# Eight 128-wide projection tiles of a two-layer hybrid block, each pair by seven block products in place of eight

## The reference

```
hn = rms_norm_2(x, norm_mix)
proj = einsum('bsd,dc->bsc', hn, w_in)
qa, ka, va, cq, ckv, kr, hc, bc, cc = split(proj)   # 384 384 384 256 128 32 256 256 256
out_a = neighbourhood_attention(norm(qa), norm(ka), va, rpb)
out_b = mla_attention(...)                # from cq, ckv, kr
out_c = bc * conv3(cc * hc)               # 3-tap convolution over the tokens
x = x + concat(out_a, out_b, out_c) normed @ w_out
x = x + expert_choice_moe(norm(x))        # 16 experts, 64 tokens each, 1024 x 1024 gate, up, down
```

## Time and profile before

| | us |
|---|---|
| median of 3 runs | 2571.51 |
| lowest and highest of them | 2571.41, 2572.59 |
| the profiled execution, its own time | 2575.35 |
| its span in the profile | 2573.5 |
| PE busy in the span | 2480.6 (96%) |
| DVE busy | 1155.5 (45%) |
| ACT busy | 477.0 (19%) |
| mean granted TensorE clock | 0.989 |

### The profile page before, as it was taken

One profiled execution on the slowest core, in us unless ns is written; L12 is line 12 of the kernel. 1 busy time (PEld: TensorE's weight loads), 2 busy tenths in 40 slices (PEclk: granted clock), 3 DMA queues, 4 the chain that ended last, 5 costly groups with the idle time before them and its releaser, 6 DMA issues.

```text
span 2573.5 us, 26561 instructions
## 1 busy us (share of the span) xinstructions
PE 2480.6 (96%) x10783; PEld 1499.0 (58%) x10783; DVE 1155.5 (45%) x2015; ACT 477.0 (19%) x1009; POOL 141.6 (6%) x237
## 2 busy tenths in 40 slices
PE   7999999999999999999999999889999999999899
PEld 3458888888888888555653333333456653333333
DVE  4667888755766643334741222111334641222112
ACT  2332121002222001233710000000224610000000
POOL 1321110000000000001100000000001000000000
PEclk9999999999999999999999999999999999999999
DMA  8535774551434225211159999999420259999998
GB/s 302 206 116 178 266 245 148 155 147 43 133 120 131 66 66 176 87 54 77 59 206 366 427 428 427 427 428 417 151 98 33 73 197 409 428 427 427 427 429 353
DMA packets 187097, 601.77 MB, mean 234 GB/s; under 512 B 8960, under 2 KB 123328, under 8 KB 161632
## 3 DMA queue, kind: packets, MB, share of 16 engines
q1 hardware_dynamic: 169072, 544.59, 54.8%
q0 software_dynamic: 16608, 51.22, 5.8%
q10 hardware_dynamic: 1296, 4.25, 0.4%
HBM read 593.74 MB, written 6.29 MB: 233 GB/s over the span
## 4 chain that ended last, share of the span: by engine, by line
PE 76%; DMA 16%; DVE 6%; issue 1%; SPq 1%; ACT 1%; DVEq 0%; ACTq 0%
DMA arena<-in_w_down 14%; PE ps L2713 9%; PE ps L2144 9%; PE ps L2269 7%; PE ps L2747 7%; PE ps L2381 5%; PE ps L2155 4%; PE ps L2617 4%; PE ps L2113 3%; PE ps L2375 3%; PE ps L2180 2%; PE ps L2038 2%; PE ps L2395 2%; PE ps L2758 2%; PE ps L2060 1%; PE ps L2552 1%
## 5 line engine op out<-in xcount | busy, mean ns | idle before, releaser
L2144 PE MATMUL ps<-arena 128*128 128x256 f32 x1280 | 278.3, 380 | 0.6 <-DVE arena L1300 0.6
L2144 PEld LDWEIGHTS ps<-arena 128*128 128x128 f32 x1280 | 242.5, 190 | 34.6 <-issue 2.0
L2713 PE MATMUL ps<-arena,first 128*64 128x512 f32 x1024 | 231.4, 593 | 12.9 <-DMA arena<-in_w_up 12.9
L2713 PE MATMUL ps<-arena 128*64 128x512 f32 x1024 | 232.4, 595 | 1.3 <-DMA arena<-in_w_up 1.3
L2747 PE MATMUL ps<-arena 128*64 128x512 f32 x896 | 210.5, 628 | 22.6 <-DMA arena<-in_w_down 21.3
L2269 PE MATMUL ps<-arena 128*128 128x256 f32 x896 | 193.8, 379 | 0.1
L2269 PEld LDWEIGHTS ps<-arena 128*128 128x128 f32 x896 | 170.1, 190 | 23.6 <-issue 0.5
L2713 PEld LDWEIGHTS ps<-arena,first 128*64 128x64 f32 x1024 | 73.3, 137 | 162.2 <-issue 136.4
L2747 PEld LDWEIGHTS ps<-arena 128*64 128x64 f32 x896 | 68.1, 144 | 162.2 <-issue 160.4
L2713 PEld LDWEIGHTS ps<-arena 128*64 128x64 f32 x1024 | 73.4, 137 | 139.8 <-issue 131.4
L2155 PE MATMUL ps<-arena 128*128 128x256 f32 x672 | 146.2, 379 | 3.0 <-DVE arena L1358 3.0
(11 more groups left out here) (465 smaller groups left out, 3179.7 us busy)
## 6 DMA issues: line engine op xcount, KB each, us to landing
arena<-in_w_gate SPq DMA_DIRECT2D x64, 2048.0 KB, 37.3
arena<-in_w_up SPq DMA_DIRECT2D x64, 2048.0 KB, 36.0
arena<-in_w_down SPq DMA_DIRECT2D x54, 2048.0 KB, 35.2
arena<-in_ffn_w SPq DMA_DIRECT2D x24, 2048.0 KB, 9.6
arena<-in_w_mod POOLq DMA_DIRECT2D x80, 512.0 KB, 5.3
arena<-in_ffn_w SPq DMA_DIRECT2D x32, 1024.0 KB, 7.9
arena<-in_w_down SPq DMA_DIRECT2D x16, 1024.0 KB, 37.9
arena<-in_w_in SPq DMA_DIRECT2D x10, 1536.0 KB, 11.6
```

The lines of the kernel that those rows point to most:

```text
L2144: ins = mm(ps[:, i % 6, 0:256], src[:, k, P * j:P * j + P], x[:, k, :], start=(k == 0), stop=(k == 3))
L2713: ins = mm(ps[CAP * half:CAP * half + CAP, bank, :], xsT[q][:, k, CAP * (e % 2):CAP * (e % 2) + CAP], wv[:, k, 512 * half:512 * half + 512 ...
```

## The change

Two tiles A and B over eight blocks of 128 input features are one 2 by 2 block product: weights a11 and a12 (the first and last four blocks of A), a21 and a22 (of B), tokens b11, b12, b21, b22 (first and last four blocks of `hnT`, first and last 256 tokens). Before, the pair takes 16 matmuls of 512 columns. After, it takes seven products of four 128x256 matmuls each, 28 in all, and sums formed by DVE. Four pairs in each layer are done so: three of convolution tiles and one of two qa tiles. The third qa tile stays as it was.

- DVE forms four token sums once per layer (`token_sums`, 1024 elements per partition each), and four weight sums per pair (`pair_sums`, 512 elements each).
- ACT copies the first two products of a pair to SBUF (256 wide). DVE combines the seven into the four quarters of the two tiles by seven adds (`pair_out`, 256 wide).
- ACT's 512-wide evictions of the eight tiles go. The squares of the two qa tiles are taken from SBUF.
- The two qa tiles are computed before ka, not after the tables.
- The token sums lie in slot 5 of the ring. So the first load of the output weights into slot 5 waits for the last product of the layer.

```diff
-        CONV_I = (0, 4, 2, 1, 5, 3)
+        PAIRS = ((4, 0, 10, 1), (4, 1, 10, 2), (4, 2, 10, 0), (1, 0, 1, 1))
+        PAIR_BANK = (4, 5, 6, 7, 0, 1, 2, 3, 4, 5, 6, 7, 3, 4, 5, 6, 7, 3, 4, 5, 6, 7, 3, 4, 0, 1, 2, 7)
...
-                if l:
-                    sp.wait_ge(r2_used[5], loads_before(5, LOADS))
-                else:
-                    sp.wait_ge(sm["f2_ps"], F2_BASE[1] + 28)
+                sp.wait_ge(sm["conv_ps"], 28 * l + 28)
                 for i, k in enumerate((6, 0)):
...
+                def pair_parts(p):
+                    if p >= 2:
+                        act.wait_ge(sm["conv_copied"], 16 * l + 4 * (p - 2) + 2)
+                    for i in range(2):
+                        act.wait_ge(sm["conv_ps"], 28 * l + 7 * p + i + 1)
+                        A(pair_q[p % 2][i], ps[:, PAIR_BANK[7 * p + i], 0:256], ACT.Copy).then_inc(sm["q_sb"], 1)
...
+                def token_sums():
+                    dve.wait_ge(sm["fin_done"], 8 * l + 8)
+                    if l:
+                        dve.wait_ge(sm["hn_ready"], 14 * l)
+                    b11, b12, b21, b22 = (hnT[:, k:k + 4, lo:lo + 256] for k in (0, 4) for lo in (0, 256))
...
+                    V.tensor_tensor(t1, b12, b11, sub).then_inc(sm["t_ready"], 1)
+                    dve.wait_ge(sm["t_ready"], done + 1)
+                    V.tensor_tensor(t2, b22, t1, sub).then_inc(sm["t_ready"], 1)
+                    V.tensor_tensor(t3, b22, b12, sub).then_inc(sm["t_ready"], 1)
+                    dve.wait_ge(sm["t_ready"], done + 2)
+                    V.tensor_tensor(t4, t2, b21, sub).then_inc(sm["t_ready"], 1)
...
+                def pair_sums(p):
+                    sa, ja, sb_, jb = PAIRS[p]
+                    for s in (sa, sb_):
+                        dve.wait_ge(r2_in[s], 16 * (l * (R2_LANDS[s] + slot_total(s)) + IN_LANDS[s]))
...
+                    if p < 2:
+                        dve.wait_ge(sm["proj_ps"], 12 * l + 2)
+                    else:
+                        dve.wait_ge(sm["conv_ps"], 28 * l + 7 * (p - 1))
+                    V.tensor_tensor(s1, a21, a22, add).then_inc(sm["ws_ready"], 1)
...
+                def pair_out(p):
...
+                    chain(V.tensor_tensor(u2_, q, product(2), add))
+                    V.tensor_tensor(u3, u2_, product(3), add)
+                    dve.wait_ge(sm["q_sb"], QSB_BASE + 8 * l + 2 * p + 2)
+                    chain(V.tensor_tensor(u4, u2_, p5, add))
+                    V.tensor_tensor(part(1, 1), shaped(u3), shaped(p5), add).then_inc(sm["conv_copied"], 1)
+                    V.tensor_tensor(part(0, 0), shaped(q), shaped(product(4)), add).then_inc(sm["conv_copied"], 1)
+                    V.tensor_tensor(part(1, 0), shaped(u3), shaped(product(5)), sub).then_inc(sm["conv_copied"], 1)
+                    V.tensor_tensor(part(0, 1), shaped(u4), shaped(product(6)), add).then_inc(sm["conv_copied"], 1)
+
+                token_sums()
+                pair_sums(0)
+                pair_sums(1)
                 dve.wait_ge(sm["proj_copied"], 12 * l + 4)
...
                 for j in range(2):
-                    dve.wait_ge(sm["conv_copied"], 6 * l + 3 * j + 3)
+                    pair_out(j)
+                    pair_sums(2 + j)
+                    dve.wait_ge(sm["conv_copied"], 16 * l + 4 * j + 4)
...
-                    V.tensor_tensor(cv[:, 2 + j, :], o, cv[:, 2 + j, :], mul).then_inc(sm["conv_sq"], 1)
+                pair_out(2)
+                dve.wait_ge(sm["conv_copied"], 16 * l + 12)
+                for j in range(2):
+                    V.tensor_tensor(cv[:, 2 + j, :], cv[:, 4 + j, :], cv[:, 2 + j, :], mul).then_inc(sm["conv_sq"], 1)
+                pair_out(3)
...
+                def product_read(n):
+                    p, i = divmod(n, 7)
+                    if i < 2:
+                        pe.wait_ge(sm["q_sb"], QSB_BASE + 8 * l + 2 * p + i + 1)
+                    else:
+                        pe.wait_ge(sm["conv_copied"], 16 * l + 4 * p + max(i - 2, 1))
...
+                def pair(p):
...
+                    for i, (w, x, s_n, t_n) in enumerate(((wa[:, 0:4], lo[:, 0:4], 0, 0), (s1, t1, 1, 1), (s2, t2, 2, 2), (s3, t3, 3, 3),
+                                                          (wa[:, 4:8], lo[:, 4:8], 0, 0), (wb[:, 4:8], t4, 0, 4), (s4, hi[:, 4:8], 4, 0))):
...
+                        for k in range(4):
+                            ins = mm(ps[:, bank, 0:256], w[:, k, :], x[:, k, :], start=(k == 0), stop=(k == 3))
+                        ins.then_inc(sm["conv_ps"], 1)
+
+                for p in range(2):
+                    pair(p)
                 pe.wait_ge(sm["c_normed"], 4 * l + 4)
+                product_read(6)
...
-                for c in range(4, 6):
-                    conv_in(c)
+                for p in range(2, 4):
+                    pair(p)
...
                 w = weights(1, 384)
-                for p in range(3):
...
+                pe.wait_ge(sm["bias_copied"], 6 * l + 2)
+                features(Q_BANK, w, 2 * P).then_inc(sm["q_ps"], 1)
```

More of the change, by code:

```diff
@@ L325, in program @@
         XT_BANK = (0, 4, 1, 6, 2, 3, 5, 7)
-        CONV_I = (0, 4, 2, 1, 5, 3)
+        PAIRS = ((4, 0, 10, 1), (4, 1, 10, 2), (4, 2, 10, 0), (1, 0, 1, 1))
+        PAIR_BANK = (4, 5, 6, 7, 0, 1, 2, 3, 4, 5, 6, 7, 3, 4, 5, 6, 7, 3, 4, 5, 6, 7, 3, 4, 0, 1, 2, 7)
+        QSB_BASE, TC_BASE, WSC_BASE = 14, 25, 92
+        pair_t = [at(20480 + 1024 * i, 1024, "p (k n) -> p k n", k=4) for i in range(4)]
+        pair_s = [[at(lo + 512 * i, 512, "p (k n) -> p k n", k=4) for i in range(4)] for lo in (34464, 42912)]
+        pair_q = [[at(15360 + 512 * j + 256 * i, 256) for i in range(2)] for j in range(2)]
+        pair_u = [at(44960 + 256 * i, 256) for i in range(3)]
         K_BANK, UP_BANK, BIAS_BANK = (3, 0, 1, 2), (4, 5, 6, 0, 1, 2, 3), (6, 0, 1, 2, 3, 4)
-        Q_BANK, V_BANK = (5, 6, 0), (1, 2, 3, 4)
+        Q_BANK, V_BANK = 0, (1, 2, 3, 4)
         T_BANK = (5, 6, 0, 1, 2, 3, 4, 5, 6, 0, 1, 2, 3, 4, 5)
@@ L813, in _ @@
                 root(0, st[:, 24:32], st[:, 16:24])
-                for c in range(4):
-                    conv_in(c)
+                for p in range(2):
+                    pair_parts(p)
                 for i in range(3):
@@ L850, in _ @@
                     ins.then_inc(sm["bias_copied"], 1)
-                for p in range(3):
-                    act.wait_ge(sm["q_ps"], 3 * l + p + 1)
-                    A(qT[:, p, :], ps[:, Q_BANK[p], :], ACT.Copy)
-                    A(sqq[:, p, :], ps[:, Q_BANK[p], :], ACT.Square).then_inc(sm["q_copied"], 1)
+                act.wait_ge(sm["conv_copied"], 16 * l + 16)
+                for p in range(2):
+                    A(sqq[:, p, :], qT[:, p, :], ACT.Square).then_inc(sm["q_copied"], 1)
+                act.wait_ge(sm["q_ps"], l + 1)
+                A(qT[:, 2, :], ps[:, Q_BANK, :], ACT.Copy)
+                A(sqq[:, 2, :], ps[:, Q_BANK, :], ACT.Square).then_inc(sm["q_copied"], 1)
                 root(2, br_, binv)
@@ L1611, in _ @@
                 chain(ins)
+                def token_sums():
[3 more added lines that the diff above has]
+                    b11, b12, b21, b22 = (hnT[:, k:k + 4, lo:lo + 256] for k in (0, 4) for lo in (0, 256))
+                    t1, t2, t3, t4 = pair_t
+                    done = TC_BASE + 4 * l
+                    V.tensor_tensor(t1, b12, b11, sub).then_inc(sm["t_ready"], 1)
[4 more added lines that the diff above has]
+                    V.tensor_tensor(t4, t2, b21, sub).then_inc(sm["t_ready"], 1)
@@ new lines, in pair_sums @@
+                def pair_sums(p):
+                    sa, ja, sb_, jb = PAIRS[p]
+                    for s in (sa, sb_):
+                        dve.wait_ge(r2_in[s], 16 * (l * (R2_LANDS[s] + slot_total(s)) + IN_LANDS[s]))
+                    wa, wb = (ring2[s][:, 0:KC * 384].rearrange("p (k n) -> p k n", k=KC)[:, :, P * j:P * j + P] for s, j in ((sa, ja), (sb_, jb)))
+                    a11, a12, a21, a22 = wa[:, 0:4], wa[:, 4:8], wb[:, 0:4], wb[:, 4:8]
+                    s1, s2, s3, s4 = pair_s[p % 2]
+                    done = WSC_BASE + 16 * l + 4 * p
+                    if p < 2:
[3 more added lines that the diff above has]
+                    V.tensor_tensor(s1, a21, a22, add).then_inc(sm["ws_ready"], 1)
+                    dve.wait_ge(sm["ws_ready"], done + 1)
+                    V.tensor_tensor(s2, s1, a11, sub).then_inc(sm["ws_ready"], 1)
+                    V.tensor_tensor(s3, a11, a21, sub).then_inc(sm["ws_ready"], 1)
+                    dve.wait_ge(sm["ws_ready"], done + 2)
+                    V.tensor_tensor(s4, a12, s2, sub).then_inc(sm["ws_ready"], 1)
@@ new lines, in pair_out, with product, part, shaped @@
+                def pair_out(p):
+                    def product(n):
+                        dve.wait_ge(sm["conv_ps"], 28 * l + 7 * p + n + 1)
+                        return ps[:, PAIR_BANK[7 * p + n], 0:256]
+                    def part(tile, half):
```

(45 more changed lines are left out.)

16 lines of the change are left out of this document (3 added, 13 removed).

## The result

The changed kernel takes 2557.07 us, median of 4 runs (2554.82 to 2559.69), where the kernel before takes 2571.95 (4 runs, 2571.41 to 2572.59). The ratio is 0.9942 by the medians; that of the runs themselves is 0.9937, 95% interval 0.9926 to 0.9949. The gain is 14.9 us; the forecast was 13.0, at 2558.5, with 2554.5 to 2563.5 as its range.

What follows compares the result with a forecast made beforehand. PE time was taken to bound the changed stretch, with DVE, ACT and DMA costs covered. Eight pairs at 1.62 us saved give 13.0 us, from 2571.51 to 2558.5 us on the median; range 2554.5 to 2563.5.

Steps and rivals of the forecast that it cites:

- Products: Convolution and qa pairs: 56 x 216.3 = 12.11 us a pair, 1.62 saved; four pairs in two layers, 13.0 us.
- Restart at each product: Rival, chance 0.04: seams between the 56 products make PE wait, at 0.58 us each 32.5 us, giving 2591.
- DVE cover: Some 29 us of sums per layer on DVE cost nothing; tightest slack 3.6 us, before the qa pair's first product.
- The rival's price: DVE late by more than its slack in pairs 2 and 3 of two layers: 8 us, 2566.5; chance 0.09.
- What moves: Per layer, ka starts 7.2 us later and the qa stretch loses two tiles, 13.7 us; va tiles 6.5 earlier.
- The moved load: Output weights into slot 5 leave at 1119.7 instead of 1039.5, first read about 1200: free.
- The expert stream: Expert loads follow PE, passing on the whole 13.0 us; rival that the gain ends there: 2571.5 at worst, chance 0.04.
- The clock: Rival after the two-column matmuls: fall gone 2554.9, one more fall per layer 2562.1; chances 0.06 and 0.05.

Runs made afterwards that it cites:

- The eighth product: Changed kernel with the last product of every pair formed twice: 2572.58 us, ratio to the kernel before 1.0004.
- the shift: Kernel before with two more 512-column matmuls ahead of the third qa tile in each layer: 2577.67 us, ratio 1.0022.
- the three-group runs: The 24 two-column matmuls split into three groups of eight: in the kernel before 2571.24 us (0.9995), in the changed kernel 2558.58 us (0.9941).

## Why the prediction was right

- **Products.** The step that carried the sum, 56 x 216.3 = 12.11 us a pair, came out at 12.09 (215.9 ns a record), and the pair saves 1.65, not 1.62: 13.2 us of trace for 13.0. The eighth product, which takes it all back, makes this the cause.
- **Restart at each product** (the slower rival): idle time before the 448 records is 0.0. Refuted: the signals are there before PE asks, and with 5.8 us more of DVE work they still were. The row that the prediction set against this rival is misread: L2269's 896 records are 28 products of 16 matmuls, not as many seams as the 56 new products have. L2144, whose 1280 records are 160 products of four matmuls, was the nearer row; its idle time is 0.6 us, so the conclusion stands.
- **DVE cover.** The first result of the third pair was expected about 1104.0 by the times of the kernel before; in the trace it ends at 1105.44, and there the first product starts 1.63 later than the first tile did: 0.2 us off. The slack of 3.6 was the one before that product; what DVE can take on is more, 5.8, because it idles 0.94 and 1.28 us for products just ahead of that result. The rival's price was wrong in kind: being late by 2 us was priced at 2 us, and it can cost more, since the clock fell behind the idle time in three places of four.
- **What moves.** ka came 7.15 us later after the projection's start (forecast 7.2), the va tiles 6.6 earlier (6.5), DVE's idle time before `p3` fell from 20.23 to 6.47 (about 6), the first load into slot 5 left at 1121.42 (about 1120). All as the walk gave.
- **The moved load.** Costed at nothing; alone it is 0.9999.
- **The expert stream.** It moved with PE: its share and rate are unchanged (1.01 and 427 GB/s from 1393.0 to 1774.5), and the layer-0 stretch from the first use of the output weights on is 603.2 us, no longer than the 606.0 before. The rival that the gain ends there is refuted.
- **The clock.** It was put down as two whole cases, all falls gone or one more per layer. In fact they come one by one: behind the two-column matmuls the clock fell in both layers of the profiles of the kernel before and of the one with its load moved, and in one layer, or none, of each profile of the changed kernel. That may be one home of the 1.6 us by which all three medians (14.9, 14.7 and 14.7 less than before) exceed the products' 13.2. Another may be the stretch from the first use of the output weights to layer 1, which no edit touches: 606.0 and 605.9 in the kernel before and with its load moved, but 603.9 and 604.4 with its two-column matmuls in groups and with the shift, and 603.2, 603.5 and 604.1 in the changed kernel. The intervals of each median hold 13.2 as well (11.3 to 18.5 in the second), and the three-group runs did not confirm the first home. So the cause of 13.2 us is shown, and that of the last 1.6 is open; that the median came out 14.9 below and not 13 is no merit of the sum.

## What to carry to other kernels

Here, with PE full and other engines with room, the seven-product scheme paid its eighth of the columns in full, since each sum and each bank was ready before PE asked. To price one elsewhere, go by the distance between matmuls of the new shape in the same trace, never by their durations. Check cover by walking the other engine's queue in order, and find its end by adding work until PE waits. Past that end a microsecond of waiting cost 1.3 to 1.4 in the stretch itself, since the clock fell with it in three places of four, and 1.5 or more on the medians. And one profile's difference (18.2) can be a quarter larger than that of the medians (14.8): compare the stretch that the edit touches, and see what identical instructions took in the others.

## What the runs showed of the hardware

Identical runs of the same kernel differ in where TensorE's granted clock falls. Behind 24 two-column float32 matmuls in a row the next two tiles took 12.26 us or 10.57 in different executions of one kernel; behind groups of eight they took 5.41 each in all four places seen. An idle time of 2.86 us cost nothing more in one layer (12.32) and 1.5 us more in the other (13.81) of one execution; 5.77 us cost 2.3 and 1.8 more (14.53 and 14.07 against 12.25). Each fall met by full work costs 1.6 to 2.3 us. Single executions of the changed kernel spread over 4.9, 5.0 and 9.5 us in its three measurements; how much of that the falls make is not shown, and they are hardly all of it: in the third, two executions with the same mean granted clock, 0.989, took 2558.93 and 2566.01 us.
